# A Trainium2 decoder step: the product-key top 16 searched among 112 pair sums and not among 256

## What is computed

```python
def one(xb):
    qh = (xb @ wq).reshape(PEER_BLOCK, PEER_HEADS, 2, PEER_DQ // 2).astype(f32)
    s1 = jnp.einsum('nhd,kd->nhk', qh[:, :, 0], subkeys[0].astype(f32))
    s2 = jnp.einsum('nhd,kd->nhk', qh[:, :, 1], subkeys[1].astype(f32))
    v1, i1 = lax.top_k(s1, PEER_TOPK)                 # 16 of 128
    v2, i2 = lax.top_k(s2, PEER_TOPK)                 # 16 of 128
    cand = (v1[..., :, None] + v2[..., None, :]).reshape(PEER_BLOCK, PEER_HEADS, PEER_TOPK * PEER_TOPK)
    sc, ci = lax.top_k(cand, PEER_TOPK)               # 16 of 256
    e = (jnp.take_along_axis(i1, ci // PEER_TOPK, axis=-1) * PEER_NKEYS
         + jnp.take_along_axis(i2, ci % PEER_TOPK, axis=-1))
    g = jax.nn.softmax(sc, axis=-1)
    ue = u[e]
    ve = v[e]
    a = jax.nn.gelu(jnp.einsum('nd,nhkd->nhk', xb, ue, preferred_element_type=f32), approximate=False)
    return jnp.einsum('nhk,nhkd->nd', (g * a).astype(x.dtype), ve).astype(x.dtype)
```

## Time and profile before

| what | value |
|---|---|
| median of 3 runs | 2361.18 us (2359.29 to 2371.97) |
| the profiled execution | 2364.91 us, span 2363.3 us |
| TensorE busy | 2133.0 us, 90% of the span |
| VectorE busy | 1359.9 us, 58% |
| ACT busy | 360.4 us, 15% |
| POOL busy | 546.1 us, 23% |
| DMA | 511.84 MB, 217 GB/s over the span |
| picks of `merge_head` | from about 815 to 951 us of the span |
| picks of `experts`, to the turn | 953 to 1199 us |

### The profile page before, as it was taken

The page is one execution under the profiler, slowest core; times in us unless marked ns, Lnnn a source line. Parts: engine busy times, 40 slices in busy tenths (PEclk is TensorE's granted clock), DMA queues, the critical chain, the costliest instruction groups (busy, mean ns, idle before and its releaser), DMA issues. The chain is left out here.

```text
span 2363.3 us, 24834 instructions
## 1 busy us (share of the span) xinstructions
PE 2133.0 (90%) x8879; PEld 1588.1 (67%) x8879; DVE 1359.9 (58%) x2817; ACT 360.4 (15%) x743; POOL 546.1 (23%) x516
## 2 busy tenths in 40 slices
PE   6958989967999989999769999997998999989997
PEld 4745677735888857677557777775666666666776
DVE  2006477752463089699997777775555455555432
ACT  1001156630010101211111221221000000000011
POOL 1001000031000000332343333333344354444200
PEclk9979999976579999999989999998999999999998
DMA  3151131032032422788689999898999999999721
GB/s 124 48 92 44 61 107 45 27 86 93 27 123 72 143 97 81 283 270 294 233 290 347 356 330 361 331 358 319 346 354 343 345 383 378 382 338 356 259 93 42
DMA packets 210225, 511.84 MB, mean 217 GB/s; under 512 B 19789, under 2 KB 106453, under 8 KB 208438
## 3 DMA queue, kind: packets, MB, share of 16 engines
q1 hardware_dynamic: 146358, 294.72, 36.0%
q0 software_dynamic: 60288, 213.96, 24.2%
q10 hardware_dynamic: 3456, 1.57, 0.2%
HBM read 460.45 MB, written 49.72 MB: 216 GB/s over the span
## 5 line engine op out<-in xcount | busy, mean ns | idle before, releaser
L1892 PE MATMUL ex_ps<-proj,ex_ring 128*128 128x320 f32 x2048 | 570.7, 442 | 54.5 <-DMA ex_ring<-in_v 54.5
L1837 PE MATMUL ex_ps<-h,ex_ring 128*128 128x320 f32 x2048 | 570.2, 435 | 8.5 <-DMA ex_ring<-in_uT 8.5
L1892 PEld LDWEIGHTS ex_ps<-proj,ex_ring 128*128 128x128 f32 x2048 | 397.5, 195 | 227.4 <-DMA ex_ring<-in_v 60.2
L1837 PEld LDWEIGHTS ex_ps<-h,ex_ring 128*128 128x128 f32 x2048 | 385.2, 191 | 160.1 <-DMA ex_ring<-in_uT 9.7
L2054 DVE TENSOR_TENSOR proj<-proj 128x320 f32<-128x320 f32 x128 | 54.4, 487 | 289.5 <-DMA proj<-scratch_a 267.1
L1999 DVE SCALAR_TENSOR_TENSOR gx_sum<-proj,gx_sum 128x1024 f32<-128x1024 f32 x120 | 154.1, 1284 | 8.4
L1745 POOL DMA_INDIRECT scores<-in_u,at_last x26 | 30.7, 1182 | 502.7 <-POOLq L1496 407.9
L1981 DVE CUSTOM_DVE_ANT_0 proj<-proj,gx_tokens 128x1024 f32<-128x1024 f32 x120 | 143.6, 1221 | 2.9 <-DMA proj<-in_u,at_upper 2.6
L1745 POOL DMA_INDIRECT proj<-in_u,at_last x76 | 87.7, 1154 | 195.6 <-DVE proj L1981 181.3
L379 PE MATMUL gate_ps<-h,work 128*128 128x260 f32 x512 | 120.6, 390 | 3.3 <-DMA work<-in_w_t 3.3
L1926 ACT ACTIVATE proj<-proj 128x2 f32<-128x2 f32 x100 | 20.4, 204 | 671.9 <-DVE proj L1981 671.8
(11 more groups left out here) (370 smaller groups left out, 2803.3 us busy)
## 6 DMA issues: line engine op xcount, KB each, us to landing
ex_ring<-in_uT SPq DMA_DIRECT2D x128, 512.0 KB, 5.7
ex_ring<-in_v SPq DMA_DIRECT2D x128, 512.0 KB, 7.8
scratch_a<-ex_gelu SPq DMA_DIRECT2D x128, 160.0 KB, 5.7
scratch_w<-proj SPq DMA_DIRECT2D x10, 2048.0 KB, 10.9
proj<-scratch_a SPq DMA_DIRECT2D x32, 640.0 KB, 12.9
proj<-scratch_w SPq DMA_DIRECT2D x32, 640.0 KB, 14.3
work<-in_w_t SPq DMA_DIRECT2D x37, 512.0 KB, 3.6
mg_ring<-in_w_q SPq DMA_DIRECT2D x32, 512.0 KB, 3.4
```

What stands on the lines that cost most here:

```text
L1837: last = nc.tensor.matmul(y[:, bank(n), 0:TD], u[:, n % UR, k, :], xn[:, k, 0:TD], start=(k == 0), stop=(k == DC - 1))
L1892: last = nc.tensor.matmul(y[:, m, 0:TD], ring[:, (E1 + e) % UR, m * P:(m + 1) * P], H[e // EG % 2][:, e % EG, :], start=(e == 0), stop=(e ...
```

## The change

The pair sums are laid out as 112 per head: 64 of the first four rows (4 x 16), then 48 of the other twelve rows' first four columns (12 x 4). One addition becomes two, the five passes of a head run over 112, and the number of a candidate is turned into row and column by two shifts, two masks and four float operations: with n the number, row = max(n >> 2 - 12, n >> 4); column = n & 15 where n >> 4 is below 4, else n & 3. Two buffers move: the integer and float parts (`cb`, `bf`) now lie behind the sums in the `attT` buffer. The estimated times that place ACT's exponentials and chunk GELUs in `experts` are changed; `EXP_HEAD` is not.

```diff
--- before.py
+++ after.py
@@ -1450,12 +1450,16 @@
     return a.sems
 
 
+FEW = 4
+CAND = FEW * PK + (PK - FEW) * FEW
+
+
 class Picker:
 
 
     def __init__(self, nc, c, small, grid, s_v, s_e, s_ex, s_t):
         self.nc, self.c, self.s_v, self.s_e, self.s_ex, self.s_t = nc, c, s_v, s_e, s_ex, s_t
-        wk, v, ix, ixf, cw, sv, ci, cb, cf = views(small, (256, 256, 256, 256, 256, 128, 128, 256, 256))
+        wk, v, ix, ixf, cw, sv, ci, cf = views(small, (256, 256, 256, 256, CAND, 128, 128, 256))
         g = grid[:, 0:SLOT * PK]
         self.sel = {
             "wk": wk.rearrange("p (a k) -> p a k", a=2),
@@ -1465,10 +1469,11 @@
             "cw": cw,
             "sv": sv.rearrange("p (h k) -> p h k", h=PH),
             "ci": ci.bitcast(U32).rearrange("p (h k) -> p h k", h=PH),
-            "cb": cb.bitcast(U32).rearrange("p (a h k) -> p a h k", a=2, h=PH),
+            "cb": g[:, PH * CAND:PH * (CAND + 4 * PK)].bitcast(U32).rearrange("p (a h k) -> p a h k", a=4, h=PH),
             "cf": cf.rearrange("p (a h k) -> p a h k", a=2, h=PH),
             "oh": g.rearrange("p (s k) -> p s k", k=PK),
-            "cd": g.rearrange("p (h a b) -> p h a b", h=PH, a=PK),
+            "cd": g[:, 0:PH * CAND].rearrange("p (h n) -> p h n", h=PH),
+            "bf": g[:, PH * (CAND + 4 * PK):PH * (CAND + 8 * PK)].rearrange("p (a h k) -> p a h k", a=4, h=PH),
         }
         self.count = 0
 
@@ -1574,8 +1579,8 @@
 
 def select_slots(nc, link, c, S, se, sel, m, nh, shifted):
 
-    wk, v, ix, ixf, cd, cw, sv, ci, cb, cf, oh = (sel[k] for k in (
-        "wk", "v", "ix", "ixf", "cd", "cw", "sv", "ci", "cb", "cf", "oh"))
+    wk, v, ix, ixf, cd, cw, sv, ci, cb, bf, cf, oh = (sel[k] for k in (
+        "wk", "v", "ix", "ixf", "cd", "cw", "sv", "ci", "cb", "bf", "cf", "oh"))
     for g in range(2 * nh):
         s = S[0:m, g, :]
         w = wk[0:m, g % 2, :]
@@ -1586,11 +1591,16 @@
         link(nc.vector.max_index(ix[0:m, g, 8:16], v[0:m, g, 8:16], w))
         yield
     vv = v[0:m, 0:2 * nh].rearrange("p (h a) k -> p h a k", a=2)
-    link(nc.vector.tensor_tensor(cd[0:m, 0:nh], vv[:, :, 0, :].unsqueeze(3).to_broadcast([m, nh, PK, PK]),
-                                 vv[:, :, 1, :].unsqueeze(2).to_broadcast([m, nh, PK, PK]), ALU.add))
+    for (a0, a1), nb, at in (((0, FEW), PK, 0), ((FEW, PK), FEW, FEW * PK)):
+        na = a1 - a0
+        done = nc.vector.tensor_tensor(
+            cd[0:m, 0:nh, at:at + na * nb].rearrange("p h (a b) -> p h a b", a=na),
+            vv[:, :, 0, a0:a1].unsqueeze(3).to_broadcast([m, nh, na, nb]),
+            vv[:, :, 1, 0:nb].unsqueeze(2).to_broadcast([m, nh, na, nb]), ALU.add)
+    link(done)
     yield
     for h in range(nh):
-        s = cd[0:m, h].rearrange("p a b -> p (a b)")
+        s = cd[0:m, h, :]
         w = cw[0:m, :]
         link(nc.vector.max(sv[0:m, h, 0:8], s))
         nc.vector.max_index(ci[0:m, h, 0:8], sv[0:m, h, 0:8], s)
@@ -1601,9 +1611,16 @@
 
     nc.vector.tensor_tensor(se[0:m, 2], sv[0:m, 0:nh], sv[0:m, 0:nh, 0:1].to_broadcast([m, nh, PK]),
                             ALU.subtract).then_inc(shifted, 1)
-    nc.vector.tensor_scalar(cb[0:m, 0, 0:nh], ci[0:m, 0:nh], 4, None, ALU.logical_shift_right)
-    link(nc.vector.tensor_scalar(cb[0:m, 1, 0:nh], ci[0:m, 0:nh], PK - 1, None, ALU.bitwise_and))
-    nc.vector.tensor_copy(cf[0:m, :, 0:nh], cb[0:m, :, 0:nh])
+    for j, (k, op) in enumerate(((4, ALU.logical_shift_right), (2, ALU.logical_shift_right),
+                                 (PK - 1, ALU.bitwise_and), (FEW - 1, ALU.bitwise_and))):
+        done = nc.vector.tensor_scalar(cb[0:m, j, 0:nh], ci[0:m, 0:nh], k, None, op)
+    link(done)
+    link(nc.vector.tensor_copy(bf[0:m, :, 0:nh], cb[0:m, :, 0:nh]))
+    by16, by4, in16, in4 = (bf[0:m, j, 0:nh] for j in range(4))
+    nc.vector.scalar_tensor_tensor(out=cf[0:m, 0, 0:nh], in0=by4, scalar=float(FEW - PK), in1=by16, op0=ALU.add, op1=ALU.max)
+    link(nc.vector.tensor_tensor(in4, in4, in16, ALU.subtract))
+    link(nc.vector.scalar_tensor_tensor(out=in4, in0=by16, scalar=float(FEW), in1=in4, op0=ALU.is_ge, op1=ALU.mult))
+    nc.vector.tensor_tensor(cf[0:m, 1, 0:nh], in16, in4, ALU.add)
     link(nc.vector.tensor_copy(ixf[0:m, 0:2 * nh], ix[0:m, 0:2 * nh]))
     yield
     n = nh * PK
@@ -1660,8 +1677,8 @@
 
         return int(us * 1165 / (2 * DC * TD))
 
-    EXP_AT = {tile_at(us): i for i, us in enumerate((74, 157, 202))}
-    DOTS_AT = [min(W0 - 1, tile_at(18 + 15.2 * k)) for k in range(PRE_CHUNKS + 1)]
+    EXP_AT = {tile_at(us): i for i, us in enumerate((70, 148, 190))}
+    DOTS_AT = [min(W0 - 1, tile_at(18 + 14.2 * k)) for k in range(PRE_CHUNKS + 1)]
     DOTS_AT += [W0 + W_EVERY * (i // 2) + (3 if i % 2 else 1) for i in range(U_CHUNKS - PRE_CHUNKS - 1)]
     with ExitStack() as ctx:
         a = Alloc(nc, ctx)
```

## The result

In a comparison of 20 runs each the changed kernel took 2350.12 us (2337.41 to 2360.20), the kernel before 2365.85 (2349.02 to 2383.55). The ratio is 0.993, with a 95% interval of 0.9911 to 0.995: 12 to 21 us less. The forecast was 17.0 us less, 2344.2 as a time against the earlier median of three runs (2361.18).

The account below looks back on a forecast made before the run. VectorE's picks were taken to end two TensorE stalls, at the experts stage's third turn and in the head lane. Savings of 13.7 + 3.3 = 17.0 us took the median from 2361.2 to 2344.2, range 2338 to 2352.

Parts of the forecast that it names:

- the two stalls: TensorE waits for VectorE: 27.59 us at the experts stage's third slot-table turn, 8.52 us for the head lane's scaled tokens.
- a head's five passes: Max, index, replace, max, index over each head's pair sums on VectorE: 2.37 us falls to about 1.62, 0.75 saved.
- pair addition, full and half: Forming the pair sums on VectorE, now two instructions: 1.1 us saved per full pick, 0.54 with half the heads.
- number to row and column, full and half: First subtraction to first one-hot on VectorE: 1.45 us longer per full pick, 1.1 longer for the half pick.
- sum in the experts stage: Searches save 15.0 us, additions 2.7, the longer way costs 4.0: third turn 13.7 us earlier, bounds 10.4 to 14.4.
- sum in the head lane: One addition and three searches stand before the scale: 1.1 + 3 x 0.75 = 3.35 us, so queries start 3.3 us earlier.
- What is late next: TensorE still reaches the third turn first, at about 1170 with 15 us to spare; tile 45 some 2 us late.
- The waits in the head lane: VectorE may wait a little for ACT's first two exponentials; the 6.17 us wait before the last one absorbs that.
- The clock: Case that TensorE's clock comes back with the shorter stalls, beyond the forecast's gain; chance 0.07.
- TensorE late at the turn: Rival: delays through ACT, SP and tile loads exceed 15 us, so TensorE ends the stretch; 2351 or 2358 us, chance 0.09.
- no narrower cost: Rival: a search over 112 costs what one over 256 does, giving 2361 us; chance 0.03.
- The last stage giving gain back: Rival: value-tile waits of 54.5 us grow, gain gone at 71.5, 2373 us or more from 83; chance 0.13.

Follow-up runs that it names:

- the two kernels in which TensorE did not wait there: Changed kernel with much shorter, wrong searches in the experts stage, 2326.11 us; changed kernel with early scale and nine chunks of dots before the turn, 2324.34 us.
- the one with ten chunks: Changed kernel with the head lane's scale one gap earlier and ten chunks of dots and adds before the third turn, not fourteen: 2327.26 us, ratio 0.982.
- the one with nine: Changed kernel with the head lane's scale one gap earlier and nine chunks of dots and adds before the third turn, not fourteen: 2324.34 us, ratio 0.9809.

## Why the prediction was right

**The bound.** That VectorE's picks end the two stalls was right at both places. Undoing the narrow search stage by stage brings each back (the wait for the scaled tokens to 8.53 us, the stretch from first tile to turn to 243.76) and leaves the other alone.

**The terms**, forecast and measured, in us:

| term | forecast | measured |
|---|---|---|
| a head's five passes | 2.37 to 1.62 | 2.37 to 1.62 |
| pair addition, full and half | 1.1 and 0.54 less | 1.13 and 0.52 less |
| number to row and column, full and half | 1.45 and 1.1 more | 1.59 and 1.25 more |
| sum in the experts stage | 13.7 | 13.28 |
| sum in the head lane | 3.35 | 3.38 |

The one term that was mis-sized is the longer way, by 0.14 and 0.15. In the full pick it is the conversion: its length was forecast well (0.43 for 0.42), but it used to start 0.21 before the next operation and is now held by a semaphore, so that the next starts 0.46 behind it (876.17 to 876.63), 0.25 more where 0.13 was counted. 2 x 0.14 + 0.15 = 0.43 accounts for the difference of 13.7 and 13.28. The four float operations take 876.63 to 877.70 = 1.07, forecast 1.06: the two that are not held are 0.29 long and the next starts 0.21 behind them, so they overlap by the 0.08 that the prediction took. The two additions overlap as well: they took 1.15 together, where 0.70 and the 0.57 of the forecast, one behind the other, would be 1.27.

**What is late next.** TensorE reached the turn 14.7 us before VectorE, forecast 15. Late tiles cost 3.02 us where 2 were forecast, and by another link: I let GELU 40's lateness pass through SP's loads to tile 45, while tile 44 waited for it directly, because from tile 43 on the program uses only four PSUM banks for tiles and tile 44 takes the one of tile 40. Hidden either way.

**The waits in the head lane.** VectorE did wait for the first two exponentials there (1.96 and 1.09 us), and the last wait, 6.17 us before, is 7.74 now: it absorbed them.

**The clock.** The forecast has no term for it, and that was right. Over the 7 us from the head lane's first query on the granted clock was 0.79 behind 8.52 us of waiting and 0.79 behind 5.14 (the window of the earlier trace rows starts 0.81 us ahead of the first query and shows 0.74), and the 256 queries took 70.58 and 70.63 us. The first tile behind the turn took 6.19 us behind 27.59 us of waiting (granted clock 0.72 from 1199.30 to 1205.50) and 6.01 behind 13.89 (0.74 from 1181.40 to 1187.40). A single tile takes 4.47 us where the clock is 1.00, so 1.7 us were lost there before the change and 1.5 after it. The chances count a clock that comes back at 0.07, and the lower end of the range, 2338, is reckoned with it; no run shows such a gain for this change. What the runs show is that the shorter stalls cost nearly as much clock as the long ones, and that the tile behind the turn took 4.47 us only in the two kernels in which TensorE did not wait there.

**The rivals.** TensorE late at the turn, and no narrower cost: refuted by the trace. The last stage giving gain back: its length differs by up to 20 us among the traces, and by 13.3 between two of the same program. Over the twelve profiled executions its length and its waits for value tiles go together; seven of them: 612.2 us with 54.5 of waits, 613.3 with 55.9, 614.6 with 53.6, 618.1 with 58.1, 622.9 with 62.0, 629.3 with 66.9, 631.8 with 66.0. The last two belong to kernels that are faster in the median than the first. So no link with the change is seen, but what starts these waits is not shown.

**The time.** 2344.2 stands 6 us under the 2350.12 measured, which is in the range; of these 4.7 are the kernel before, whose median of 20 is 2365.85 and not 2361.18. Against its own reference the gain is 15.7, with 17.0 inside the interval.

## What to carry to other kernels

When one engine is 90% busy, look for the few places where it waits for another and count that engine's unbroken stretch back to its last wait: within it every microsecond counted in full here (14.0 us of padding moved the turn by 14.0), up to the moment at which the busy engine arrives. What is saved beyond that counts only if the busy engine waits for the same engine again soon behind, as here for the first one-hot (2.32 us). Before making the late engine's work cheaper, ask which of it need not be there at all: moving five chunks to where VectorE waits anyway (with the scale a gap earlier) gave more, 2350 to 2324, than the narrower search, 2366 to 2350. And compare traces up to a marker in front of any stage whose length changes from run to run; a single pair here would have put the gain at 4.7 us.

## What the hardware showed unexpectedly

At the turn a short stall cost TensorE as much clock as a long one. Windows of 7 us just behind the turn; the columns are length, busy us of PE, PEld (its weight loads), DVE, ACT and POOL, granted clock, DMA share, GB/s. First the changed kernel behind 13.89 us, then the one with ten chunks behind 2.28, then the one with nine behind no wait:

```profile
1181.00:1188.00 7.00, 6.43 (x19) 4.09 (x17) 6.79 (x12) 0.64 (x2) 3.96 (x3) 0.75 0.78 265
```

```profile
1164.00:1171.00 7.00, 6.66 (x22) 4.65 (x23) 6.82 (x14) 0.10 (x1) 2.72 (x4) 0.76 0.93 362
```

```profile
1160.00:1167.00 7.00, 7.00 (x37) 5.49 (x36) 6.25 (x12) 1.44 (x3) 0.07 (x1) 1.00 0.45 109
```

The first tile behind the turn took 6.19 us behind 27.59 us of waiting, 6.01 behind 13.89 and 6.16 behind 2.28, but 4.47 behind none. In all traces with a wait there it took 5.54 to 7.07 us, in no order of the wait: 7.01 belongs to 7.47 us, 7.07 to 12.62. So shortening this wait brought no clock back, and only its end did, 1.1 to 2.6 us at once.

It is no rule for every short wait. This window lies behind 2.30 us of waiting for a tile, some 20 us in front of the turn, in the kernel with the wide search in the head lane only:

```profile
1164.40:1171.40 7.00, 7.00 (x26) 5.02 (x27) 6.72 (x19) 2.06 (x4) 3.94 (x3) 1.00 0.66 238
```

And in the two executions of the changed kernel TensorE waited 2.32 and 2.40 us for the first one-hot; the next tile took 4.47 us in one and 6.16 in the other. What decides between the two is not shown.
